# First mixer of a fused forward pass: its norm, gating and mixing moved beside its input products

## The reference, cut to what matters

```python
def rms_norm(x, g):
    y = x * rsqrt(mean(x * x, axis=-1, keepdims=True) + 1e-6)
    return y * g

def sgu_mixer(h, w_in, b_in, g_v, w_s, b_s, w_out):   # h = rms_norm(x, norm_mix_g[0])
    z = gelu(h @ w_in + b_in)                # 512 x 2048, exact gelu
    u, v = split(z, 2)                       # gates u, values v
    v = rms_norm(v, g_v)
    v = v.reshape(B, 4, 128, 16, 64)         # blocks of 128 tokens, 16 groups of 64 features
    v = einsum('gts,bnsgc->bntgc', tril(w_s), v) + b_s
    return (u * v.reshape(B, 512, 1024)) @ w_out
```

## Time and profile before

| | us |
|---|---|
| median of 3 runs | 3002.13 (3001.97 to 3002.72) |
| the profiled execution | 3002.88 |
| its span in the trace | 3001.0 |
| PE busy | 2806.3 (94%) |
| DVE busy | 1567.8 (52%) |
| ACT busy | 1038.0 (35%) |
| POOL busy | 717.0 (24%) |
| mean granted TensorE clock | 0.956 |

### The profile page before, as it was taken

The page is one execution under the profiler, slowest core; times in us unless marked ns, Lnnn a source line. Parts: engine busy times, 40 slices in busy tenths (PEclk is TensorE's granted clock), DMA queues, the critical chain, the costliest instruction groups (busy, mean ns, idle before and its releaser), DMA issues. The chain is left out here.

```text
span 3001.0 us, 37578 instructions
## 1 busy us (share of the span) xinstructions
PE 2806.3 (94%) x13754; PEld 2226.4 (74%) x13754; DVE 1567.8 (52%) x1934; ACT 1038.0 (35%) x1845; POOL 717.0 (24%) x665
## 2 busy tenths in 40 slices
PE   6889999799999999999999888899999888999999
PEld 4678888655788878888777765588888655788887
DVE  3267774374643467774467555554432446654432
ACT  3323332224333333333234535432222227532221
POOL 0031111232551451111201445231112004421100
PEclk9999999989988999999999989899999988999999
DMA  3212223311100012233322012132223210122233
GB/s 123 76 57 91 98 96 91 109 50 42 57 22 19 2 55 93 98 96 88 97 79 83 23 46 55 32 100 98 98 88 97 90 50 1 36 98 97 93 90 105
DMA packets 79532, 218.95 MB, mean 73 GB/s; under 512 B 21806, under 2 KB 21934, under 8 KB 79023
## 3 DMA queue, kind: packets, MB, share of 16 engines
q1 hardware_dynamic: 78974, 213.94, 22.9%
q10 hardware_dynamic: 432, 3.33, 0.3%
HBM read 215.14 MB, written 2.10 MB: 72 GB/s over the span
## 5 line engine op out<-in xcount | busy, mean ns | idle before, releaser
L311 PE MATMUL psum<-rounded,high_r 128*128 128x512 f32 x3040 | 1204.9, 396 | 56.0 <-DVE rounded L272 26.9
L313 PE MATMUL psum<-rounded,high_r 128*128 128x512 f32 x3040 | 1193.4, 393 | 0.0
L315 PE MATMUL psum<-rounded,ring_low 128*128 128x512 f32 x3040 | 1192.3, 392 | 0.0
L331 ACT ACTIVATE high_r<-ring 128x1024 fp32r<-128x1024 f32 (+2 forms) x432 | 420.3, 973 | 1453.0 <-PE psum L315 1431.3
L336 DVE TENSOR_TENSOR ring_low<-ring,high_r 128x1024 fp32r<-128x1024 f32 (+2 forms) x430 | 522.0, 1214 | 591.1 <-ACT high_r L331 589.9
L311 PEld LDWEIGHTS psum<-rounded,high_r 128*128 128x128 f32 x3040 | 576.8, 190 | 213.7 <-issue 64.9
L315 PEld LDWEIGHTS psum<-rounded,ring_low 128*128 128x128 f32 x3040 | 576.9, 190 | 121.8
L313 PEld LDWEIGHTS psum<-rounded,high_r 128*128 128x128 f32 x3040 | 577.5, 190 | 118.1 <-issue 1.0
L768 DVE TENSOR_TENSOR arena<-psum,inverse 128x512 f32<-128x512 f32 x176 | 121.5, 691 | 314.3 <-PE psum L315 314.1
L624 POOL CAST rounded<-rows 128x512 f32 (+1 forms) x88 | 53.8, 611 | 785.6 <-DVE rows L773 785.6
L626 POOL TENSOR_TENSOR rounded<-rows,rounded 128x512 f32 (+1 forms) x88 | 115.7, 1314 | 13.2 <-POOL rounded L624 11.9
(11 more groups left out here) (383 smaller groups left out, 3008.9 us busy)
## 6 DMA issues: line engine op xcount, KB each, us to landing
ring<-in_up SPq DMA_DIRECT2D x176, 512.0 KB, 3.3
ring<-in_down SPq DMA_DIRECT2D x64, 384.0 KB, 3.1
ring<-in_down SPq DMA_DIRECT2D x64, 320.0 KB, 2.9
ring<-in_even_in SPq DMA_DIRECT2D x36, 512.0 KB, 3.5
ring<-in_sgu_in SPq DMA_DIRECT2D x16, 512.0 KB, 3.3
ring<-in_even_out SPq DMA_DIRECT2D x16, 384.0 KB, 3.1
ring<-in_qkv SPq DMA_DIRECT2D x12, 512.0 KB, 3.5
ring<-in_sgu_out SPq DMA_DIRECT2D x8, 512.0 KB, 3.3
```

Source lines behind the costliest of these rows:

```text
L311: nc.tensor.matmul(psum[:, m, :], high_r[:, r % HIGHS, blk], x_high, start=(k0 + k == 0), stop=False)
L313: nc.tensor.matmul(psum[:, m, :], high_r[:, r % HIGHS, blk], x_low, start=False, stop=False)
L315: mm = nc.tensor.matmul(psum[:, m, :], ring_low[:, r % R, blk], x_high, start=False, stop=end)
L331: nc.scalar.activation(high_r[:, r % HIGHS, 0:nk * P], ring[:, r % R, 0:nk * P], ACT.Copy).then_inc(unit_high, 1)
```

## The change

The mixer becomes one phase, in one block with the feed-forward layer behind it (`with joined(): sgu()`), written out by hand.

- **Loading.** ACT's queue loads x in 8 transfers, each with a semaphore of its own; SP's queue loads the vectors, two weight units, the constants, two more units and the mixing weights without waiting for anything.
- **Inputs.** ACT and DVE split gain times x (`Handed`, L380 and L385) as the tiles land; the split inputs are not divided by the norm. DVE multiplies each product tile by the reciprocal instead (`scale`), ahead of ACT's Gelu.
- **x's norm.** ACT squares x behind the splits; POOL adds the 8 squares; one matmul with ones sums over features, after unit 1.
- **Order of the outputs.** The host's packing of the weights puts the 8 value tiles first. ACT takes Gelu and a second pass with the gain g_v (`gained`); PE transposes a value tile after the following unit; ACT keeps it. POOL squares and sums the values.
- **Values' norm.** Per token: 4 one-column matmuls after unit 9, root and reciprocal on 128x4, then DVE and POOL scale two token blocks each of the turned values.
- **Mixing** after units 11 and 12, the transposes back after units 13 and 14, gates multiplied in on DVE; the output's split is shared by ACT with POOL (tiles 0 to 3) and DVE (tiles 4 to 7).
- sgu_in's loops are unrolled. POOL masks the mixing weights.

The diff, cut to its core (inside `sgu`):

```diff
-                self.unrolled = name == "even_in"
+                self.unrolled = name in ("sgu_in", "even_in")
...
                 @block.sync
                 def _(sp):
+                    sp.dma_start(vec[:, :], dram["vec"]).then_inc(vec_loaded, 16)
+                    load_unit(sp, st, 0, 0)
+                    load_unit(sp, st, 0, 1)
+                    sp.dma_start(const[:, :], dram["const"]).then_inc(const_loaded, 16)
+                    load_unit(sp, st, 0, 2)
+                    load_unit(sp, st, 0, 3)
+                    sp.dma_start(span(WC, 4), dram["sgu_ws"]).then_inc(ws_loaded, 16)
+                    load_stream(sp, name)
...
                 @block.tensor
                 def _(pe):
...
+                    def beside(n):
+                        if n == 1:
+                            pe.wait_ge(const_loaded, 16)
+                            pe.wait_ge(added, KD - 1)
+                            nc.tensor.matmul(psum[:, 4, :], con("ones"), square_sum[:, :], start=True, stop=True).then_inc(totalled, 1)
+                        if n == 2:
+                            turn_v(0)
+                        if 2 <= n <= KD:
+                            turn_v(n - 1)
+                        if n == 9:
+                            pe.wait_ge(v_summed, KD - 1)
...
+                        if n in (11, 12):
+                            for pair in range(4 * (n - 11), 4 * (n - 11) + 4):
+                                mix(pair)
+                        if n in (13, 14):
+                            for j in range(4 * (n - 13), 4 * (n - 13) + 4):
+                                turn_y(j)
+                    products(pe, name, two_parts(XI, XR), scaled, handed.ready(pe), after_unit=beside)
+                @block.gpsimd
+                def _(pool):
+                    for i in range(1, KD):
+                        pool.wait_ge(squared, i + 1)
+                        if i >= 2:
+                            pool.wait_ge(added, i - 1)
+                        nc.gpsimd.tensor_tensor(square_sum[:, :], square_sum[:, :], arena[:, VT + i, :], ALU.add).then_inc(added, 1)
...
+                    for c in (2, 3):
+                        nc.gpsimd.tensor_scalar(vtv[:, c, :], vtv[:, c, :], per_token[0][:, c:c + 1], None, ALU.mult).then_inc(v_scaled_pool, 1)
+                    for j in range(4):
+                        pool.wait_ge(y_high, j + 1)
+                        nc.gpsimd.tensor_tensor(y_low_parts[:, j, :], arena[:, U + j, :], y_high_parts[:, j, :].bitcast(F32),
+                                                ALU.subtract).then_inc(y_low_pool, 1)
...
+                @block.scalar
+                def _(act):
+                    def gelu(n):
+                        act.wait_ge(scaled, n + 1)
+                        if 2 <= n < KD:
+                            act.wait_ge(v_squared, n - 1)
+                        nc.scalar.activation(home(n), zs(n), ACT.Gelu, bias=col("sgu_b", n + KD if n < KD else n - KD)).then_inc(taken, 1)
+                        if n < KD:
+                            act.wait_ge(taken, n + 1)
+                            if n >= 2:
+                                act.wait_ge(v_turned, n - 1)
+                            nc.scalar.activation(arena[:, VG + n % 2, :], home(n), ACT.Copy, scale=col("sgu_gv", n)).then_inc(gained, 1)
+                    def beside(n):
+                        if n == 1:
+                            act.wait_ge(guarded, 1)
+                            nc.scalar.activation(inverse[:, 1, :], inverse[:, 0, :], ACT.Sqrt).then_inc(rooted, 1)
+                            gelu(0)
+                        if 1 <= n < TILES:
+                            gelu(n)
+                        if n == 2:
+                            keep_v(0)
+                        if 2 <= n <= KD:
+                            keep_v(n - 1)
...
+                    for n in range(TILES):
+                        if n == TILES - 1:
+                            gelu(n)
+                        next_split(act, split_high, n + 2)
+                        if n < TILES - 1:
+                            beside(n)
+                    for j in range(4, KD):
+                        high(j)
...
                 @block.vector
                 def _(dve):
+                    def scale(n):
+                        dve.wait_ge(unit_done, st.first + n + 1)
+                        if n >= 2:
+                            dve.wait_ge(taken, n - 1)
+                        nc.vector.tensor_tensor(zs(n), psum[:, n % 4, :], inverse[:, 0, :], ALU.mult).then_inc(scaled, 1)
...
+                    for n in range(TILES):
+                        if n == TILES - 1:
+                            scale(n)
+                        next_split(dve, split_low, n + 2)
+                        beside(n)
+                    make(KD - 1)
+                    for j in range(4, KD):
+                        low(j)
...
-        sgu()
+        with joined():
+            sgu()
...
-    d["sgu_in"] = blocks(a["sgu_w_in"][0])
+    d["sgu_in"] = blocks(a["sgu_w_in"][0], order=np.concatenate([np.arange(8, 16), np.arange(8)]))
```

219 lines of the change are left out of this document (165 added, 54 removed).

## The result

| us | before | changed |
|---|---|---|
| median of the paired runs | 3002.05 (4 runs, 2989.89 to 3002.72) | 2953.67 (4 runs, 2943.1 to 2964.02) |
| ratio, 95% interval | | 0.9848 [0.9801, 0.9895] |
| the profiled execution | 3002.88 | 2948.1 |
| its span | 3001.0 | 2946.3 |
| PE / DVE / ACT / POOL busy | 2806.3 / 1567.8 / 1038.0 / 717.0 | 2777.5 / 1554.6 / 1047.8 / 762.0 |

The kernel is 1.5% faster; the forecast was 2956. The span is 54.7 us shorter, but only 43.1 of these lie in the code that was changed.

A forecast was written before the change was run, and what follows sets the result against it. PE, full in steady streams, idles in the mixer waiting for other engines. Start to 46.5, stream 80.0, into sgu_out 10.6 end at 137.1 against 183.6: 46.5 us off 3002.9 gives 2956, range 2950 to 2963, chance 0.60.

The forecast's parts named there:

- Landing: Start of the mixer: x's last tile lands at 16 us beside the queued weights, bounds 8.3 and 18.6.
- Rival A: Start: x lands first, tiles at 8 to 10 us, few clock losses; 2947 to 2948 us in all; chance 0.13.
- First two units: Start of PE's products: first at about 10 us, unit 0 done at 18.9, unit 1 at 25.5.
- x's norm: After unit 1: additions end at 29.3, PE stops 3.8 us, sum takes 0.8, chain behind it ends at 39.5.
- Unit 3: End of the start: 5.4 us plus 1.1 for the clock after PE passes two transposes at 40.0; done at 46.5.
- Units 4 to 15: Stream with transposes, sums and mixing inside: 80.0 us, no waits but 1.0 before mixing; ends at 126.5.
- DVE beside POOL: Values' scaling before mixing: by a port-lock rule DVE's and POOL's scalings would queue, mixing some 2 us later; not in the sum.
- Into sgu_out: After unit 15 to the end of sgu_out's first unit: 10.6 us with a 3 us wait; done at 137.1.
- the clock term: In sgu_out's first unit: after PE's 3 us wait the last four tiles run at half clock, 4 x 1.28 us.
- B: Value tiles: POOL and DVE's split collide, a new wait of 1.6 us for 7 tiles; 14 more, 2970; chance 0.12.
- C: Start: x lands last (18.6), POOL's additions all collide, a second clock loss; 2966 us; chance 0.12.
- D: Value tiles: a table load at each Gelu switch, 3.1 us for each of 15 tiles; 3003 and above; chance 0.03.

The follow-up runs named there:

- x_one: Changed kernel with x loaded in one transfer (rows of 16 KB) instead of eight (rows of 2 KB); median 2956.38 us, ratio to before 0.9834.
- sq_early: Changed kernel with ACT squaring each tile of x directly behind its split instead of all eight behind the eighth; median 2951.79 us, ratio to before 0.9839.
- best1: Changed kernel with x in one transfer, squares behind each split, sum after unit 0, mixing weights masked behind the values' squares; 2948.54 us, ratio to before 0.9846.

## Why the prediction was right, and where it was not

The mechanism was as forecast: the mixer ends 43.1 us sooner (44.7 in the second trace) where 46.5 were forecast. Step by step, with the working as in the prediction:

- **Landing: wrong.** 16 forecast for the last tile of x, upper bound 18.6; measured 19.5, outside the bounds. I had a likely reason (short rows) but not its size. The bound used 426 GB/s; with the 409 from 4 to 18 us it would be 19.2. x_one shows that one transfer with long rows brings x to 9.3. Rival A, x first, at 0.13, was what that kernel does and this one does not.
- **First two units.** First product at 10, measured 10.13. Unit 0 done at 18.9, measured 23.6: 3.5 us are the landing. The rest is that the last two tiles landed 0.6 us apart and both were multiplied at the lower clock, 0.43 us a matmul from 20.53 on, after stops of 1.0 to 1.6 us for L385. The prediction had read from the earlier trace rows that the clock holds through a stop of 1.05 us; here stops of 1.00, 1.28 and 1.64 stood one after the other ahead of its fall. The first six products (10.13 to 12.83) also follow each other at 0.43 us, where the granted clock in the rows is 1.00; no run shows why.
- **x's norm: mis-sized.** The additions ended at 34.0, not 29.3: 3.2 for their late start, 1.5 for their pace (11.66 for seven, 1.67 each with hops, where I had 1.37): two of them met an L336 and took 2.12 and 2.27 instead of 1.28, where I had counted one such meeting, at 0.5. The stop of 3.8 us was measured as 3.67, which is luck: unit 1 was late by 5.0 us, the additions by 4.7. The sum took 2.04, not 0.8: 1.02 even at full clock (sq_early), the rest is the lower clock. The chain behind it took 9.1, not 9.9.
- **Unit 3** was done at 50.6 (as the rows are cut), not 46.5. These 4.1 us are the whole error of the start.
- **Units 4 to 15: right.** 80.2 measured, 80.0 forecast. The second loss of the clock that I had counted ahead of it didn't come. The wait before mixing was 0.20, not 1.0, and the per-token sums 0.95, not 0.4.
- **DVE beside POOL.** DVE's two scalings took 1.67 together while POOL's 6.29 ran (lines above), 2.27 in best1 at most. POOL's second scaling, the one beside them, took 3.46 against 2.85 for its first; no run shows DVE's two without POOL. The Trainium skill (SBUF — State Buffer, section Who interferes with whom) says that a tensor_scalar on DVE can take the port pair shared with GpSimd, one engine blocking the other for the whole instruction. The 2 us that the prediction estimated from this did not come. For DVE instructions with two SBUF operands the trace agrees with what the Trainium skill says in the same section, and the price was higher than mine: 5.56 instead of 1.23 beside one long POOL instruction, with the end 1.1 us after POOL's in all four kernels in which the two met.
- **Into sgu_out.** 9.7 measured, 10.6 forecast. The stop was 1.73 instead of 3, with the clock lost behind it. That the clock term came true is luck too: after the same stop it stayed up in five of nine traces, the second one of this kernel among them, and the stretch then takes 8.1.

Errors of 4.1, 0.2 and -0.9 give 3.4, the difference between 140.5 and 137.1. The total came out nearer than the mark by luck, for a reason that the prediction didn't have: 2956.4 + 3.4 - 11.6 = 2948.2, the profiled execution. "What follows is the same code in both" was true, but not that it takes the same time. Of the 11.6 us 7.8 are in units 112 to 128 and 4.2 in units 240 to 256, where the same work ran at a higher granted clock (0.95 against 0.92, 0.93 against 0.90); the rest nets to -0.4.

**Rivals.** B (a new wait at every value tile) is refuted: no L858 after the second waits. C asked for a landing above 18, which came, but its further loss did not, since the early start was worth 11.7 us at unit 3. D is refuted: Gelu's table was loaded twice in the whole mixer (behind the two roots), and never between units 3 and 9.

**What stays open.** What picks a stage's clock level. The levels repeat between the two traces of each kernel, and don't follow the place in time alone. The four executions of the changed kernel took 2943.1, 2948.1, 2959.2 and 2964.0 us at mean granted clocks of 0.966, 0.964, 0.959 and 0.957. The kernel before is not tied to its level either: over all sessions its executions took 2985.7 to 3003.3. So of the gain of 48 us in the medians only the mixer's 43 to 45 are the change's for certain. The forecast's term for it would have been 0 with a spread of about 12 either way.

## What to carry to other kernels

When a division by a norm is linear in the products, divide the products: here it let PE start under the norm, and undoing it alone cost 13.6 us in this order of work. The rest of the gain was in small steps that no longer stand in a row behind barriers; but a step moved into a full stream saves nothing if it would have covered the stream's end. Compare kernels by a mark at the end of the changed code as well as by the total, since untouched stages can shift by more than the change of interest; and look at the clock just ahead of the mark, since a stop of 1.7 us cost 1.6 more in four of nine traces.
